# RWKV-7 chunk inverse in a trunk-step kernel: each level works on the 32 of 64 columns that it alters

## The chip, the cores and the metric

The kernel runs on one core of a Trainium2 chip. Five engines work side by side and meet only at semaphores: PE (TensorE, matrix products from SBUF into PSUM; its weight loads are listed as PEld), DVE (VectorE), ACT (ScalarE), POOL (GpSimd) and SP, which here only issues DMAs. The metric is the device time of one execution in microseconds; lower is better. The time before is the median of three runs.

## The reference, cut to what matters

The reference is one inference step of a two-layer hybrid trunk. Layer 1 mixes tokens with a bidirectional RWKV-7 scan and a Mamba-2 scan. The part that matters is the RWKV scan:

```python
def wkv_scan(r, w, kk, a, k, v, S0, reverse):
    ...
    def step(S, inp):
        r_t, w_t, a_t, b_t, k_t, v_t = inp
        sa = jnp.einsum('bhvk,bhk->bhv', S, a_t)
        S = S * w_t[:, :, None, :] + sa[..., None] * b_t[:, :, None, :] + v_t[..., None] * k_t[:, :, None, :]
        return S, jnp.einsum('bhvk,bhk->bhv', S, r_t)
    S, ys = lax.scan(step, S0.astype(f32), xs, reverse=reverse)
```

There are 8 heads of 64 channels, 640 tokens and two directions. All data is float32.

## The kernel before, in words

The token loop is not run token by token. The 640 tokens are cut into NC = 10 chunks of 64. Inside a chunk the effect of the tokens on one another is a 64x64 triangular matrix (a "gram", masked), and the chunk is solved by the inverse of identity minus that matrix. A job is one direction (d = n % 2) of one pair of heads (j = n // 2): 8 jobs, each with 10 chunks and 2 heads (e). The head decides which half of the partitions holds a matrix (ROWS), so the arrays that matter, X_ (the inverse), XT_ (its transpose) and V_ (a product), are 128 partitions x 10 chunks x 64 columns. The chunks are worked on in two groups g of 5, 320 columns each.

The inverse is built by doubling. Level 0 is read straight from the masked gram. Levels lev = 1 to 5 join neighbouring blocks of width w = 2 ** lev. One level of one group is four steps:

- piece "v" on PE (line 2413): V = gram x X, ten products of 64x64 by 64x64, into PSUM bank VT(g); then on DVE (line 2684) the result times the 0/1 mask wlev(d, lev), which keeps the blocks that this level fills in, into V_.
- piece "xt" on PE: for levels under 5 ten products XT x V that are accumulated onto XB(g) in PSUM (line 2422), and ten products V x XT into VT(g) (line 2426); then on ACT (line 2580) the whole of XB(g) is copied to X_, and on DVE (line 2689) VT(g) is added to XT_.

Every product helper call has the line of `mm`, L226, in the profile, so only the accumulated product has a line of its own (L2422). A float32 product shows as two pairs of a weight load and a matmul. The mask keeps in each level only columns whose place in a block of 2w is in one half: half of the 64 columns of V and X change, and the other half of the columns of XT.

The order of the work is written out by hand. `wkv_order` (line 2239) yields the pieces for all engines alike; each engine goes through the same list and does its share, so every engine's queue follows that order. Each job has 20 slots, v and xt of two groups for 5 levels. After each slot the table BESIDE adds pieces of the next job (`to` = 1: lora, scan, prod, vt, gram, atok, bktok, lkv, x0, which prepare it) and of the job before (`to` = -1: uw, phi, z, chain, yi, ye, which use its inverse). Line 2671 evicts and masks the gram on DVE, lines 2643 to 2662 are the prod pieces on DVE, lines 2786 and 2788 make level 0 of the next job on POOL, and line 2400 (x0) turns it into XB. L2722 is a step of the state chain on DVE. L2548, L2561, L2562 and L2568 are ACT's copies in the pieces prod, vt and atok. PE takes PSUM banks 4 to 6 in turn for the pieces beside the levels; `claim` waits until the bank has been read.

Constants come from one array in DRAM. `shape_constants` fills it on the host, `const_columns` gives its layout; SP loads four of them and the start state before the RWKV phase (lines 3087 and 3088), and DVE and POOL wait for 16 * 5 on wkv_loaded.

## Time and profile before

| | |
|---|---|
| median of 3 runs | 1996.38 us (1993.99 to 1997.78) |
| the profiled execution: span from first to last instruction | 2001.7 us; no other time is given for it |
| PE busy, share of the span | 1921.7 us, 96% |
| DVE busy | 1071.2 us, 54% |
| ACT busy | 717.5 us, 36% |
| POOL busy | 140.2 us, 7% |
| mean granted TensorE clock | 0.983 |

Busy time of an engine is time in which one of its instructions runs. Matmuls are pipelined, so busy PE time is not time at its peak rate. A group in a table is a line, an engine and an operation, with what it writes and reads and the shape as partitions x elements. The chain of waits is followed back from the last instruction, at each step to what released it.

### The profile page before, as it was taken

The numbers are of one execution on the slowest core, as the hardware profiler recorded it, in microseconds if no ns is written. First come the engines' busy times: TensorE is split into PE (matmuls) and PEld (weight loads), VectorE is DVE, ScalarE is ACT, GpSimd is POOL, SyncE is SP. The second block draws the span as 40 slices with busy tenths as digits, with TensorE's granted clock in tenths as the row PEclk, the third lists the DMA queues.
The fourth block names the chain that finished last, engine by engine and source line by source line (L and its number), as shares of the span: only waits on it lengthen the run. The fifth ranks groups of instructions, "written<-read, shape, count | busy, mean of one in ns | idle before, by whom it ended". The sixth has DMA issues, their size and how long they took to land.

```text
span 2001.7 us, 41374 instructions
## 1 busy us (share of the span) xinstructions
PE 1921.7 (96%) x18397; PEld 1700.8 (85%) x18397; DVE 1071.2 (54%) x1976; ACT 717.5 (36%) x1313; POOL 140.2 (7%) x138
## 2 busy tenths in 40 slices
PE   5998999999999999999999889999999999999997
PEld 2795444899999999999998678888659999999997
DVE  3226754475555563245475776766547555556223
ACT  2323554353333351133345744444214333334211
POOL 2000000000000000000001523322000000000000
PEclk7999999999999999999999999999899999999999
DMA  9123738312221223232221000000211222122322
GB/s 339 56 85 119 273 112 301 119 58 85 85 70 58 85 58 87 59 105 70 64 84 41 7 3 4 4 4 4 91 43 43 85 84 84 52 76 59 87 64 76
DMA packets 142065, 164.25 MB, mean 82 GB/s; under 512 B 2512, under 2 KB 107136, under 8 KB 141888
## 3 DMA queue, kind: packets, MB, share of 16 engines
q1 hardware_dynamic: 138736, 150.29, 23.3%
q0 software_dynamic: 3152, 11.32, 1.5%
q8 instruction: 145, 2.38, 0.5%
q14 instruction: 32, 0.26, 0.0%
HBM read 157.85 MB, written 3.75 MB: 81 GB/s over the span
## 4 chain that ended last, share of the span: by engine, by line
PE 87%; DVE 6%; DMA 2%; POOL 2%; ACT 1%; issue 1%; POOLq 0%; DVEq 0%; SPq 0%
PE ps L226 82%; DMA ring<-in_ada_w 2%; POOL work L2786 1%; PE ps L2422 1%; DVE ring L2671 1%; PE ps L1280 1%; DVE work L498 1%; POOL work L2788 1%; PE ps L347 1%; PE ps L2027 1%; DVE small L1415 0%; PE ps L2400 0%; PE ps L462 0%; DVE work L2689 0%; DVE work L2684 0%
## 5 line engine op out<-in xcount | busy, mean ns | idle before, releaser
L226 PE MATMUL ps<-x_hi_r,w_lo 128*128 128x320 f32 (+3 forms) x2240 | 519.7, 307 | 0.4 <-issue 0.4
L226 PE MATMUL ps<-x_hi_r,w_hi 128*128 128x320 f32 (+2 forms) x1792 | 428.9, 311 | 0.9 <-issue 0.9
L226 PE MATMUL ps<-x_lo_r,w_hi 128*128 128x320 f32 (+2 forms) x1792 | 424.9, 308 | 0.0
L226 PEld LDWEIGHTS ps<-x_hi_r,w_lo 128*128 128x128 f32 (+1 forms) x2240 | 372.4, 186 | 2.0 <-issue 0.5
L226 PEld LDWEIGHTS ps<-x_lo_r,w_hi 128*128 128x128 f32 x1792 | 305.6, 188 | 0.0
L226 PEld LDWEIGHTS ps<-x_hi_r,w_hi 128*128 128x128 f32 x1792 | 303.8, 188 | 1.4 <-issue 1.3
L226 PE MATMUL ps<-work 64*64 64x64 f32 (+9 forms) x3322 | 285.0, 281 | 17.0 <-ACT work L1344 6.7
L226 PEld LDWEIGHTS ps<-work 64*64 64x64 f32 (+5 forms) x3322 | 177.7, 152 | 97.6 <-issue 64.1
L678 DVE SCALAR_TENSOR_TENSOR work<-ps,par,work 128x511 f32<-128x511 f32 (+1 forms) x188 | 103.3, 550 | 254.5 <-ACT work L840 244.6
L840 ACT ACTIVATE work<-ps,par 128x640 f32<-128x640 f32 x88 | 78.0, 886 | 372.5 <-PE ps L226 372.5
L718 ACT ACTIVATE w_hi<-ring 128x1024 fp32r<-128x1024 f32 (+1 forms) x152 | 135.8, 938 | 206.9 <-DMA ring<-in_ffn_down 182.7
L729 DVE TENSOR_TENSOR w_lo<-ring,w_hi 128x1024 fp32r<-128x1024 f32 (+1 forms) x152 | 158.6, 1078 | 87.0 <-ACT w_hi L718 87.0
L226 PE MATMUL ps<-g_lo,w_hi 128*128 128x320 f32 (+2 forms) x704 | 174.6, 309 | 0.0
L226 PE MATMUL ps<-work,ring 64*64 64x64 f32 (+3 forms) x2368 | 122.0, 238 | 7.3 <-DVE work L2689 3.3
L226 PEld LDWEIGHTS ps<-g_lo,w_hi 128*128 128x128 f32 x704 | 121.4, 188 | 0.0
L226 PEld LDWEIGHTS ps<-work,ring 64*64 64x64 f32 (+2 forms) x2368 | 94.9, 142 | 30.8 <-issue 25.5
L448 DVE SCALAR_TENSOR_TENSOR h<-ps,mods,h 128x512 f32<-128x512 f32 (+2 forms) x76 | 34.9, 494 | 140.6 <-PE ps L226 140.5
L226 PE MATMUL ps<-x_lo_r,w_lo 128*128 128x320 f32 (+2 forms) x416 | 108.1, 310 | 0.0
L680 DVE SCALAR_TENSOR_TENSOR work<-ps,par,work 128x511 f32<-128x511 f32 (+1 forms) x188 | 103.4, 550 | 6.7
L226 PE MATMUL ps<-x_hi_r,w_in_hi 128*128 128x320 f32 (+1 forms) x384 | 88.4, 312 | 0.5 <-issue 0.4
L226 PE MATMUL ps<-x_lo_r,w_in_hi 128*128 128x320 f32 (+1 forms) x384 | 86.8, 307 | 0.0
L226 PE MATMUL ps<-ring,cond 128*32 128x512 f32 x384 | 56.0, 668 | 19.9 <-DMA ring<-in_ada_w 19.8
(383 smaller groups left out, 2534.1 us busy)
## 6 DMA issues: line engine op xcount, KB each, us to landing
ring<-in_ada_w SPq DMA_DIRECT2D x24, 2048.0 KB, 8.1
ring<-in_ffn_up SPq DMA_DIRECT2D x44, 1024.0 KB, 7.3
ring<-in_ffn_down SPq DMA_DIRECT2D x16, 1408.0 KB, 6.9
ring<-in_l_w_in SPq DMA_DIRECT2D x11, 1024.0 KB, 5.2
ring<-in_l_w_out SPq DMA_DIRECT2D x4, 2048.0 KB, 7.9
ring<-in_l_w_in SPq DMA_DIRECT2D x3, 2048.0 KB, 9.5
h<-in_xT POOLq DMA_DIRECT2D x1, 2560.0 KB, 14.7
out_yT<-work POOLq DMA_DIRECT2D x2, 768.0 KB, 4.0
```

The costliest lines, as they stand in the source:

```text
L226: return pe.matmul(out, lhsT, rhs, start=first, stop=last)
L347: ins = pe.matmul(ps_all[:, 1024 * pair + heads * c:1024 * pair + heads * c + heads], squares[:, P * c:P * c + P], col, start=first and c ...
L448: ins = dve.scalar_tensor_tensor(h(m, x, y), psum(u % 2, x, y), gate(m, c), h(m, x, y), ALU.mult, ALU.add)
L498: ins = dve.scalar_tensor_tensor(hn(t, x, y), h(t, x, y), gain(t, c), bank(6 + p)[:, x - a:y - a], ALU.mult, ALU.mult)
L678: ch(dve.scalar_tensor_tensor(acc(a + 1, b), psrc(a, b - 1), w0, acc(a + 1, b), ALU.mult, ALU.add))
L680: ins = dve.scalar_tensor_tensor(acc(a, b - 1), psrc(a + 1, b), w2, acc(a, b - 1), ALU.mult, ALU.add)
L718: act.activation(wh_b[:, SLOT * (f % 2) + w * part:SLOT * (f % 2) + w * part + w], ring[:, SLOT * (n % RING) + w * part:SLOT * (n % RING) ...
L729: dve.tensor_tensor(wl_b[:, at:at + w], ring[:, at:at + w], wh_b[:, SLOT * (f % 2) + w * part:SLOT * (f % 2) + w * part + w].bitcast(F32), ...
L840: act.activation(tile(cacc, 2 * (m % 2) + half), spair(n % 3, cut=up_cut(n)), ACT.Identity, bias=pc(f"ffn_b{l}", half * FT + m), scale=cw( ...
L1280: ins = pe.transpose(bank(4)[:, P * kt:P * kt + P] if kt < 4 else bank(5, P), pb[:, P * kt:P * kt + P], ident[:, :])
L2027: pe.matmul(out(hd), xtok[:, 512 * c + 64 * hd:512 * c + 64 * hd + 64], M_b[:, 1024 * x + P * hd:1024 * x + P * hd + P], start=hd % 4 < 2, ...
L2422: x = pe.matmul(XB(g)[p0:p1, c - 5 * g, :], XT_(n)[q0:q1, c, :], V_[q0:q1, c, :], start=False, stop=True, skip_group_check=True)
```

## The change

In each level the products, masks, additions and copies work on the half of the columns that the level alters, taken by a strided view: with w = 2 ** lev, 32 / w runs of w neighbouring columns, w apart. On V and X it is side d, on XT the other side. The other columns of V_ now keep old values. As the left operand of the products V is still loaded with all 64 columns, so rows of the V x XT product that belong to the other side hold values that must not be added; the addition therefore becomes one with a per-partition factor rsel(d, lev) of 0 or 1. V_ is set to zero once, before the first job. The constant rsel (10 columns) is new, with a DMA of its own, and the waits on wkv_loaded go to 16 * 6.

```diff
--- before.py
+++ after.py
@@ -65,7 +65,7 @@
     at, n = {}, 0
     for name, w in (("ident", P), ("blk", P), ("rotA", P), ("rotB", P), ("cosA", NL), ("sinA", NL),
                     ("cosB", NL), ("sinB", NL), ("gmask", 2 * P), ("wmask", 2 * P), ("wlev", 12 * 64),
-                    ("id64", 64), ("reset65", 650), ("reset", NT), ("sel6", 6 * P), ("rmask", 8)):
+                    ("id64", 64), ("rsel", 10), ("reset65", 650), ("reset", NT), ("sel6", 6 * P), ("rmask", 8)):
         at[name] = (n, w)
         n += w
     return at, n
@@ -2167,7 +2167,7 @@
         assert 2688 + 3 * NT + 4 * NT + 512 >= W0 + 4 * NT
         c_reset2, c_wmask, c_wlev, c_id64 = tk(650), tk(2 * P), tk(12 * 64), tk(64)
         assert 2688 + 3 * NT + 4 * NT + 512 + 650 + 2 * P + 13 * 64 <= W0 + 8 * NT
-        pv_b, _ = tk(36), tk(24)
+        pv_b, c_rsel, _ = tk(36), tk(10), tk(14)
         RH_b, X_b, XT_b = tk(4 * NT), tk(2 * NT), tk(2 * NT)
         cum_b, swx_b = tk(650), tk(650)
         V_b, W_b, RP_b, PH_b, ZP_b = tk(NT), tk(NT), tk(NT), tk(NT), tk(NT)
@@ -2189,6 +2189,14 @@
         V_, W_, RP_, PH_, ZP_ = c10(V_b), c10(W_b), c10(RP_b), c10(PH_b), c10(ZP_b)
         en65, ep65, sw65 = c10(en_b), c10(cum_b), c10(swx_b)
         wlev = lambda d, lev: c_wlev[:, 384 * d + 64 * lev:384 * d + 64 * lev + 64]
+        rsel = lambda d, lev: c_rsel[:, 5 * d + lev - 1:5 * d + lev]
+
+        def half_columns(ap, lev, side):
+
+            w = 1 << lev
+            if len(ap.shape) == 2:
+                return ap.rearrange("p (b h w) -> p b h w", h=2, w=w)[:, :, side, :]
+            return ap.rearrange("p c (b h w) -> p c b h w", h=2, w=w)[:, :, :, side, :]
         HALF5, THIRD = ((0, 5), (5, 10)), ((0, 4), (4, 8), (8, 10))
         ROWS = ((0, 64), (64, P))
         pv = lambda n, c, w=1: pv_b[:, 12 * (n % 3) + c:12 * (n % 3) + c + w]
@@ -2410,7 +2418,8 @@
                     for c in range(5 * g, 5 * g + 5):
                         for e in range(2):
                             (p0, p1), (q0, q1) = ROWS[e], ROWS[1 - e]
-                            ins = mm(pe, VT(g)[q0:q1, c - 5 * g, :], G_(n)[p0:p1, c, e, 0:64], X_(n)[p0:p1, c, :])
+                            ins = mm(pe, half_columns(VT(g)[q0:q1, c - 5 * g, :], lev, d), G_(n)[p0:p1, c, e, 0:64],
+                                     half_columns(X_(n)[p0:p1, c, :], lev, d))
                     ins.then_inc(sg("wkv_v"), 1)
                 elif kind == "xt":
                     lev, g = i
@@ -2419,11 +2428,13 @@
                         if lev < 5:
                             for e in range(2):
                                 (p0, p1), (q0, q1) = ROWS[e], ROWS[1 - e]
-                                x = pe.matmul(XB(g)[p0:p1, c - 5 * g, :], XT_(n)[q0:q1, c, :], V_[q0:q1, c, :],
+                                x = pe.matmul(half_columns(XB(g)[p0:p1, c - 5 * g, :], lev, d), XT_(n)[q0:q1, c, :],
+                                              half_columns(V_[q0:q1, c, :], lev, d),
                                               start=False, stop=True, skip_group_check=True)
                         for e in range(2):
                             q0, q1 = ROWS[1 - e]
-                            ins = mm(pe, VT(g)[q0:q1, c - 5 * g, :], V_[q0:q1, c, :], XT_(n)[q0:q1, c, :])
+                            ins = mm(pe, half_columns(VT(g)[q0:q1, c - 5 * g, :], lev, 1 - d), V_[q0:q1, c, :],
+                                     half_columns(XT_(n)[q0:q1, c, :], lev, 1 - d))
                     if lev < 5:
                         x.then_inc(sg("wkv_x"), 1)
                     ins.then_inc(sg("wkv_t"), 1)
@@ -2577,7 +2588,8 @@
                 elif kind == "xt" and i[0] < 5:
                     lev, g = i
                     act.wait_ge(sg("wkv_x"), 8 * n + 2 * (lev - 1) + g + 1)
-                    act.activation(X_(n)[:, 5 * g:5 * g + 5, :], XB(g), ACT.Copy).then_inc(sg("wkv_xu"), 1)
+                    act.activation(half_columns(X_(n)[:, 5 * g:5 * g + 5, :], lev, d), half_columns(XB(g), lev, d), ACT.Copy)\
+                        .then_inc(sg("wkv_xu"), 1)
                 elif kind == "uw":
                     act.wait_ge(sg("wkv_uw"), 3 * n + i + 1)
                     c0, c1 = THIRD[i]
@@ -2592,7 +2604,7 @@
                     act.activation(gates_b[i // 2][:, :], spair(i // 2 % 2), ACT.Copy).then_inc(sg("gate_read"), 1)
 
         def wkv_dve(dve, ch, scan_end):
-            dve.wait_ge(sg("wkv_loaded"), 16 * 5)
+            dve.wait_ge(sg("wkv_loaded"), 16 * 6)
             many = lambda ap, k: ap.unsqueeze(1).to_broadcast([P, k, ap.shape[1]])
             links = 0
             for kind, n, i in wkv_order():
@@ -2626,6 +2638,7 @@
                     dve.scalar_tensor_tensor(part, part, pc("gnorm", t), factor_b[:, a:a + 320], ALU.mult, ALU.mult)
                 elif kind == "x0" and n == 0 and i == 1:
                     ch(dve.memset(pv_b[:, 12:36], 1.0))
+                    ch(dve.memset(V_b, 0.0))
                 elif kind == "scan":
                     dve.wait_ge(sg("wkv_sw"), 2 * n + 2)
                     dve.tensor_tensor_scan(cum_b[:, :], c_reset2[:, :], swx_b[:, :], 0.0, ALU.mult, ALU.add)\
@@ -2681,12 +2694,16 @@
                 elif kind == "v":
                     lev, g = i
                     dve.wait_ge(sg("wkv_v"), 10 * n + 2 * (lev - 1) + g + 1)
-                    dve.tensor_tensor(V_[:, 5 * g:5 * g + 5, :], VT(g), many(wlev(d, lev), 5), ALU.mult).then_inc(sg("wkv_vm"), 1)
+                    mask = half_columns(wlev(d, lev), lev, d)
+                    dve.tensor_tensor(half_columns(V_[:, 5 * g:5 * g + 5, :], lev, d), half_columns(VT(g), lev, d),
+                                      mask.unsqueeze(1).to_broadcast([P, 5, mask.shape[1], mask.shape[2]]), ALU.mult)\
+                        .then_inc(sg("wkv_vm"), 1)
                 elif kind == "xt":
                     lev, g = i
                     dve.wait_ge(sg("wkv_t"), 10 * n + 2 * (lev - 1) + g + 1)
-                    x = XT_(n)[:, 5 * g:5 * g + 5, :]
-                    dve.tensor_tensor(x, x, VT(g), ALU.add).then_inc(sg("wkv_tu"), 1)
+                    x = half_columns(XT_(n)[:, 5 * g:5 * g + 5, :], lev, 1 - d)
+                    dve.scalar_tensor_tensor(x, half_columns(VT(g), lev, 1 - d), rsel(d, lev), x, ALU.mult, ALU.add)\
+                        .then_inc(sg("wkv_tu"), 1)
                 elif kind == "phi":
                     dve.wait_ge(sg("wkv_phi"), 3 * n + i + 1)
                     c0, c1 = THIRD[i]
@@ -2741,7 +2758,7 @@
         def wkv_pool(pool, store_scan):
             pl = Chain(pool, "pool_chain")
             pl.n = 1
-            pool.wait_ge(sg("wkv_loaded"), 16 * 5)
+            pool.wait_ge(sg("wkv_loaded"), 16 * 6)
             for kind, n, i in wkv_order():
                 j, d = n // 2, n % 2
                 if kind == "lora":
@@ -3083,7 +3100,7 @@
                     sp.dma_start(c_reset1, part_of_const("reset65")).then_inc(sg("reset_loaded"), 16)
                     sp.wait_ge(sg("ssd_tok"), 5)
                     sp.wait_ge(sg("ssd_skip"), 4)
-                    for name, to in (("reset65", c_reset2), ("wmask", c_wmask), ("wlev", c_wlev), ("id64", c_id64)):
+                    for name, to in (("reset65", c_reset2), ("wmask", c_wmask), ("wlev", c_wlev), ("id64", c_id64), ("rsel", c_rsel)):
                         sp.dma_start(to, part_of_const(name)).then_inc(sg("wkv_loaded"), 16)
                     sp.dma_start(s0_b, t_in["wkv0"]).then_inc(sg("wkv_loaded"), 16)
                     sp.wait_ge(sg("wkv_yi"), 2 * JOBS)
@@ -3146,6 +3163,7 @@
             lev.append(lower if (d == 0) != (b == 0) else upper)
     put("wlev", np.concatenate(lev, 1))
     put("id64", s == t)
+    put("rsel", np.concatenate([(s % (2 << b) >= (1 << b)) == (d == 1) for d in range(2) for b in range(1, 6)], 1))
     put("reset65", np.tile((np.arange(650) % 65 != 0)[None], (P, 1)))
     put("reset", np.tile((np.arange(NT) % P != 0)[None], (P, 1)))
     sel6, rmask = np.zeros((P, 6, P)), np.zeros((P, 8))
```

## Rows read from the trace of the kernel before

**Rows 1.** The page: busy time of PE, and the granted clock in 40 slices.

```profile
PE 1921.7 (96%) x18397; PEld 1700.8 (85%) x18397; DVE 1071.2 (54%) x1976; ACT 717.5 (36%) x1313; POOL 140.2 (7%) x138
...
PEclk7999999999999999999999999999899999999999
```

**Rows 2.** Busy time in stretches; after POOL: granted clock, DMA share, GB/s.

```profile
1261.00:1295.40 34.40, 32.50 (x983) 28.50 (x983) 23.88 (x58) 16.89 (x42) 9.92 (x7) 1.00 0.02 4
...
1231.90:1235.30 3.40, 3.40 (x62) 3.16 (x64) 1.39 (x4) 2.44 (x5) 0.00 (x0) 0.51 0.00 0
```

**Rows 3.** Chain of waits, 1261 to 1296 us: start us, us, what.

```profile
1262.92 0.40 DVE work L2689
...
1264.05 0.40 DVE work L2684
...
1267.57 0.32 ACT work L2580
...
1273.48 0.40 DVE work L2684
...
1274.07 0.39 DVE work L2689
...
1279.65 0.62 PE ps L2400 x14
```

**Rows 4.** Chain of waits, 1190 to 1400 us: L2647 in three jobs.

```profile
1226.98 0.74 DVE work L2647
...
1261.69 0.73 DVE work L2647
...
1295.79 0.73 DVE work L2647
```

**Rows 5.** Groups by line: duration ns min/median/max, starts; the second by form.

```profile
L2684 DVE TENSOR_TENSOR work<-ps,work x80: 460/491/494, 1146.7 to 1415.1; 128x320 f32<-128x320 f32 x80
...
L448 DVE SCALAR_TENSOR_TENSOR h<-ps,mods,h 128x128 f32<-128x128 f32 x44 | 14.1, 344 | 7.5 <-PE ps L226 7.4
...
L2580 ACT ACTIVATE work<-ps x64: 417/439/443, 1150.2 to 1413.6; 128x320 f32<-128x320 f32 x64
...
L2585 ACT ACTIVATE work<-ps x24: 278/385/387, 1181.3 to 1420.7; 128x256 f32<-128x256 f32 x16, 128x128 f32<-128x128 f32 x8
```

**Rows 6.** DVE in order of time: start us, us, line, operation.

```profile
1258.49 0.28 DVE L2694 TENSOR_TENSOR work<-ps,work 128x128 f32<-128x128 f32 x1
1258.69 0.28 DVE L2695 TENSOR_TENSOR work<-ps,work 128x128 f32<-128x128 f32 x1
```

**Rows 7.** PE and weight loads in order of time: start us, us, line, operation.

```profile
1218.15 0.14 PEld L2422 LDWEIGHTS ps<-work 64*64 64x64 f32 x2
...
1218.21 0.14 PEld L2422 LDWEIGHTS ps<-work 64*64 64x64 f32 x2
...
1439.12 1.20 PEld L347 LDWEIGHTS ps<-blk,sqb 128*128 128x128 f32 x10
...
1213.34 0.63 PE L226 MATMUL ps<-work,ring 64*64 64x64 f32 x15
1213.90 0.81 PE L226 MATMUL ps<-work 64*128 64x320 f32 x4
...
1202.26 1.16 PE L226 MATMUL ps<-work 64*128 64x128 f32 x16
1203.35 0.62 PE L226 MATMUL ps<-work,ring 64*64 64x64 f32 x14
```

**Rows 8.** SP's issues, one landing, and DVE at the phase's start, in order of time.

```profile
1092.34 2.02 SPq L3087 DMA_DIRECT2D work<-in_const  x4
...
work<-in_const SPq DMA_DIRECT2D x1, 32.0 KB, 3.9
...
1130.62 1.01 DVE L2618 SCALAR_TENSOR_TENSOR merged<-work,par,ps 128x384 f32<-128x384 f32 x2 [1.50 <-PE ps L2032]
...
1146.70 0.49 DVE L2684 TENSOR_TENSOR work<-ps,work 128x320 f32<-128x320 f32 x1 [2.66 <-PE ps L226]
```

## The prediction

> **What bounds the kernel now.** I read the page first, then the stretches of single jobs, then the chain of waits through one job, then single groups. The page says that PE is busy nearly all the time at nearly full clock [rows 1]. The reader should not stop there. The change touches only the level loop of the RWKV inverse, whose masks run from 1146.7 to 1415.1 us [rows 5], some 275 us or 14% of the span, for eight jobs. One job's stretch of 34.4 us has PE busy for 32.5 us and DVE for 23.9 us [rows 2], which still looks like a PE bound. The chain of waits through the same stretch says otherwise [rows 3]. From 1262.92 to 1279.65 us it runs over DVE (the prod pieces, with one L2689 and one L2684 queued among them), ACT (with one L2580), the gram products on PE, DVE again (L2684 and L2689 between two gram evictions) and POOL. Only from 1279.65 us on, where PE takes up x0 (L2400), is it PE alone, until the next prod stretch begins a little before the L2647 at 1295.79 us [rows 4], some 14 us. So a job is some 20 us of a mixed chain and 14 us of PE, and the change has to be priced in both. The start of one prod piece in successive jobs gives the pitch of a job: 34.71 and 34.10 us [rows 4].
>
> **Weights, masks and vector work, part by part.** Per job there are 5 levels and 2 groups: 10 masks (L2684), 10 additions (L2689), 8 copies (L2580), and 20 blocks of products.
>
> *Mask.* L2684 on 320 columns takes 491 ns [rows 5]. In the chain it advances the queue by 0.40 us [rows 3]. The same kind of operation on 128 columns takes 0.28 us and the next one starts 0.20 us later [rows 6]. From 128 to 320 columns the step grows by 0.20 us in 192 columns, 1.04 ns a column. 160 columns: 0.20 + 32 x 1.04 ns = 0.23 us of queue, 0.31 us long. Each mask gives 0.17 us.
>
> *Addition.* It becomes an operation with a per-partition factor. L448 is such an operation: 128 columns take 344 ns [rows 5] against 280 ns without the factor [rows 6], so the factor costs 64 ns. 160 columns: 0.29 us of queue. Each addition gives 0.11 us, not 0.17.
>
> *Copy.* L2580 takes 439 ns; another PSUM copy on ACT takes 278 ns at 128 and 385 ns at 256 columns [rows 5], 0.84 ns a column. 160 columns: 0.305 us. Each gives 0.13 us.
>
> All three now read and write runs of 2, 4, 8, 16 or 32 numbers. No row at hundreds of columns has runs so short. Bounds: at best nothing on top; at worst the halving is given back in full, for which the nearest rows are the 320-column ones. I take nothing on top: the 128-column rows read PSUM in runs of 64 out of 128 (lines 2694 and 2695) and still cost less per column than the contiguous 320 ones, so a gap between runs by itself is free. The Trainium skill (Vector Engine (DVE) Microarchitecture Reference, 5.2 Measured stream behaviour on trn2) has full rate for runs of at least two adjacent words that start on 8 bytes, and 1.3 to 2.5 ns a column otherwise. By it all runs here are free, level 1 included; no row here shows it.
>
> *Products.* Half the columns stream, but each product still loads 64 weight columns. Weight loads of a level block follow each other at 0.06 us (1218.15, 1218.21), and ten loads of 128 weight columns whose products have 2 columns take 1.20 us, 0.112 us each [rows 7]. So a load sets a pitch of its own of about 0.112 / 2 = 0.056 us for 64 weight columns even when almost nothing streams. The pitch inside a block should stay: zero for all 1600 passes (8 jobs x 5 levels x 2 groups x 5 chunks x 2 passes, for v and for xt). What does shrink is the end of a block before work of another tile shape. After 64-column products the next block starts 0.15 us after the last product's start (1213.34 + 0.63 - 0.22 = 13.75, then 13.90). After 128-column ones it is 0.20 us (1202.26 + 1.16 - 0.27 = 3.15, then 3.35) [rows 7]. That is 0.86 ns a column, so 27 ns less at 32 columns. By the order table about 9 of the 20 blocks stand before a piece of another shape (lora, atok, bktok, gram, a turned vt), about 3 of them in the stretch where PE alone is the chain: 0.08 us a job. Bounds: 0 and 9 x 27 = 0.24 us.
>
> *What is added.* A load of ten columns in SP's queue beside the four constant loads at 1092 us [rows 8]; DVE's first operation of this phase starts at 1130.62 us, so some 30 us cover it. If that cover were gone it would cost one landing, 3.9 us, once. The clearing of V stands in DVE's queue before the first mask, where DVE idles 2.66 us [rows 8]; it needs at most the 0.73 us of a 640-column operation such as L2647 [rows 4], and without that cover it costs just this. The queue waits for one semaphore more of the same DMA group; nobody else is behind it.
>
> **The sum.** On the chain of one job lie the addition just before the prod stretch and one inside it (2 x 0.11), one mask (0.17), one copy (0.13, in the three jobs of even number after job 0, whose chain it is; I did not find it on that of the odd ones), and one mask and one addition ahead of the last gram eviction (0.28, of which I take 0.20, because the eviction then waits for its product). With the PE term that is 0.22 + 0.17 + 0.20 + 0.08 = 0.67 us, and 0.80 us with the copy. Seven such stretches (three with the copy): 7 x 0.67 + 3 x 0.13 = 5.1 us. Job 0's first levels and the last job's tail, where levels follow one another with little beside them: 0.4 us. Total 5.5 us.
>
> Against it stands the clock. The chip granted 0.51 of full speed, the lower of its levels (1.2 of 2.4 GHz), for 3.4 us at 1231.9 us, just after a stretch in which PE had mostly waited for DVE [rows 2]. The job with that stretch is 34.71 us and the next one, without, is 34.10 us [rows 4]: some 0.6 us each time (the two jobs differ in direction, so this is rough). Halved streams leave PE less to do around these waits. I charge one more such stretch: 0.7 us. Net 4.8 us.
>
> The profiled execution's span is 2001.7 us; no other time of it is given. It lies 5.3 us above the median of 1996.4 us, so the sum reads 2001.7 - 4.8 = 1996.9 for it, and 1996.4 - 4.8 = 1991.6 us for the median. About 0.2% (4 us) is what a measurement of this kernel can tell from no change, and my sum lies just beyond that.
>
> **Rivals.**
>
> *Absorbed (chance 0.27).* The chain moves to what is late next: ACT's queue before the gram products, POOL's three long operations, the gram products themselves. None of these shrinks. For it: the piece before each saved one often waited for PE. Against it: the saved pieces stand on the chain itself [rows 3]. Only the additions and masks of the prod stretch would count, about 0.3 us in 7 jobs: 2 us, so 1994.4 us.
>
> *The clock takes it back (0.10).* If nearly every job gets two stretches of 3.4 us at the lower level, some 9 more than now, 9 x 0.6 = 5.4 us cancel the gain; twice that price gives 5 us too many: 1996 to 2001 us. For it: the kernel already falls there in some jobs. Against: before 1279.65 us PE is not the chain, so a slow clock costs little.
>
> *Strided products are slow (0.08, the slower side).* Place: the reads of the moving operand and the writes to PSUM in the 1600 passes. A pass has 0.059 us, and 32 columns at 0.86 ns need 0.028 us. So streaming at half rate would be hidden completely under the weight load. It decides from 0.059 + 5.5 / 1600 = 0.0624 us a pass, 1.95 ns a column, 2.3 times today's price. At four times (0.11 us a pass) it costs 1600 x 0.051 = 82 us: 2073 us. If only the runs of two (level 1, 320 passes) suffer, 16 - 4.8: 2008 us. No row shows a product on short runs. The PSUM page of the Trainium skill (PSUM — Partial Sum Buffer, Specifications (TRN2)) says that any non-contiguous access pattern slows matmuls significantly, with 8-byte lines. By its word this rival would be the forecast; by its 8-byte line a run of two is whole, and nothing is lost. No run yet shows which.
>
> *Products do halve (0.05).* That would be the full meaning of "32 of 64 columns": the weight load is not the limit, and a pass falls from 0.059 to about 0.04 us. In the 14 us of PE chain lie 9 blocks, 90 passes a job: 90 x 0.019 x 8 = 14 us more, 1978 us. Against it: the 2-column products at 0.112 us [rows 7].
>
> **How the numbers follow.** Forecast as summed: 0.50. Its own spread is 1988 to 1995 us (PE ends from 0 to 0.24 us a job, low-clock stretches from 0 to 4, short runs from free to half given back). About two thirds of it lie beyond 4 us. Faster: two thirds of 0.50, all of 0.05, and a third of the absorbed case, about 0.45. Slower: 0.08, a third of the clock case and a little for unknown costs, 0.13. The rest, 0.42, is within 0.2%. The range 1986.5 to 1998.5 takes in the forecast, the absorbed case and most of the clock case and leaves out the two extremes.
>
> **What the next profile would show.** Mask about 0.31 us, addition about 0.38 us, copy about 0.305 us, at every level alike; if level 1 is longer, short runs cost something. Weight loads inside level blocks still at 0.059 us; a larger pitch is the strided rival, a smaller one the last. Block ends at 0.12 instead of 0.15 us. Pitch of a job about 0.7 us shorter, the chain still over the prod pieces, gram and POOL. More stretches at half clock in the level loop speak for the clock rival. I am wrong if the three vector times are as said and the jobs are not shorter, or if the weight-load pitch moves at all.

## The result, and the profile after

The changed kernel takes 2012.2 us (median of 6, 2004.4 to 2028.7) against 1997.5 us for the kernel before (median of 6): a ratio of 1.0075, 95% interval 1.0047 to 1.0103. It is some 15 us slower, where 1991.6 us and a range up to 1998.5 us were forecast. The profiled execution took 2008.95 us, with a span of 2007.1 us.

The page of the kernel after, busy time and granted clock in 40 slices, beside [rows 1]:

```profile
PE 1932.5 (96%) x18397; PEld 1713.9 (85%) x18397; DVE 1053.3 (52%) x1977; ACT 709.1 (35%) x1313; POOL 140.0 (7%) x138
...
PEclk8999999999999999999999988988899999999999
```

DVE and ACT do less, as they should. PE, whose products shrank, is busy for 10.8 us more, and there are slices with an 8 in the clock in the level loop. The busy time of PE grew where the same instructions ran at a lower clock; in the jobs at full clock, below, it shrank a little (31.8 us against 32.2 in the second).

The changed groups by line of the kernel after, duration in ns min/median/max, beside [rows 5]:

```profile
L2698 DVE TENSOR_TENSOR work<-ps,work x80: 294/324/330, 1144.4 to 1420.7; 128x160 f32<-128x160 f32 x80
...
L2705 DVE SCALAR_TENSOR_TENSOR work<-ps,work x80: 369/384/387, 1148.0 to 1422.2; 128x160 f32<-128x160 f32 x80
...
L2591 ACT ACTIVATE work<-ps x64: 286/314/332, 1148.1 to 1419.1; 128x160 f32<-128x160 f32 x64
```

Mask, addition and copy have nearly the durations forecast (0.31, 0.38, 0.305 us), and the levels hardly differ: their means lie at 313 to 325, 379 to 384 and 302 to 321 ns, with 325, 384 and 320 ns at level 1, where the runs have 2 numbers. So short runs cost next to nothing. The vector side of the change did what it promises.

Now the loop by jobs, each window from the first mask of a job to the first of the next. First the kernel after, all eight jobs; after the length come the busy times of PE, PEld, DVE, ACT and POOL, then the granted clock, third from the end:

```profile
1144.40:1178.20 33.80, 29.21 (x792) 25.80 (x794) 19.24 (x42) 14.04 (x36) 12.36 (x13) 0.85 0.03 11
1178.20:1211.70 33.50, 31.78 (x969) 28.20 (x971) 21.93 (x58) 15.87 (x42) 9.88 (x7) 1.00 0.02 4
1211.70:1247.70 36.00, 33.51 (x958) 30.34 (x958) 22.01 (x59) 14.04 (x36) 11.79 (x9) 0.86 0.01 4
1247.70:1280.90 33.20, 31.60 (x969) 28.11 (x969) 21.06 (x57) 15.88 (x42) 9.88 (x7) 1.00 0.02 4
1280.90:1320.20 39.30, 37.60 (x958) 34.12 (x958) 22.06 (x58) 14.19 (x36) 11.79 (x9) 0.74 0.01 3
1320.20:1353.80 33.60, 31.76 (x969) 28.17 (x969) 21.09 (x57) 15.89 (x42) 9.89 (x7) 1.00 0.02 4
1353.80:1392.70 38.90, 36.74 (x962) 33.34 (x962) 22.14 (x58) 14.19 (x36) 11.79 (x9) 0.78 0.01 4
1392.70:1422.60 29.90, 25.77 (x768) 24.36 (x764) 13.59 (x42) 10.13 (x25) 4.61 (x3) 0.83 0.02 4
```

The same windows of the kernel before, the second to the sixth:

```profile
1179.50:1214.00 34.50, 32.20 (x969) 28.16 (x969) 24.34 (x57) 16.87 (x42) 9.92 (x7) 1.00 0.02 4
1214.00:1248.70 34.70, 31.87 (x958) 28.33 (x958) 24.13 (x58) 15.05 (x36) 11.82 (x9) 0.95 0.02 4
1248.70:1282.70 34.00, 32.10 (x969) 28.16 (x969) 23.54 (x56) 16.88 (x42) 9.92 (x7) 1.00 0.02 4
1282.70:1318.20 35.50, 33.05 (x958) 29.51 (x958) 24.11 (x58) 15.05 (x36) 11.84 (x9) 0.90 0.02 4
1318.20:1352.60 34.40, 32.23 (x969) 28.19 (x969) 23.69 (x57) 16.87 (x42) 9.91 (x7) 1.00 0.02 4
```

The pattern is plain once the clock column is read. Where the clock is 1.00 the jobs are shorter after: 33.5, 33.2 and 33.6 us against 34.5, 34.0 and 34.4. Where it isn't, they are longer: 36.0 against 34.7 and 39.3 against 35.5. Here is the lower clock by itself in the kernel after, with the stretch just before one fall:

```profile
1224.70:1228.10 3.40, 2.14 (x88) 1.84 (x82) 3.40 (x7) 0.32 (x1) 1.91 (x2) 1.00 0.00 0
1228.10:1238.30 10.20, 9.06 (x166) 8.36 (x166) 5.62 (x17) 2.22 (x5) 0.00 (x0) 0.50 0.01 3
1296.30:1316.80 20.50, 19.70 (x384) 18.04 (x384) 9.41 (x27) 5.39 (x14) 4.63 (x4) 0.50 0.01 3
1371.40:1388.50 17.10, 17.10 (x324) 15.75 (x326) 6.80 (x19) 4.98 (x13) 4.18 (x3) 0.50 0.01 3
```

In the kernel before, the stretch ahead of the fall in [rows 2], and its three other low stretches:

```profile
1228.50:1231.90 3.40, 1.63 (x66) 1.39 (x66) 3.40 (x9) 0.04 (x1) 1.68 (x2) 1.00 0.02 5
...
1156.80:1160.20 3.40, 3.36 (x94) 3.06 (x96) 1.77 (x4) 0.98 (x3) 0.00 (x0) 0.51 0.02 5
...
1300.20:1307.00 6.80, 6.32 (x100) 5.74 (x102) 3.78 (x12) 2.48 (x5) 0.00 (x0) 0.50 0.01 2
1402.60:1412.80 10.20, 8.14 (x151) 7.71 (x155) 3.17 (x8) 2.25 (x6) 1.83 (x2) 0.50 0.01 2
```

Before, the loop has 23.9 us at the lower level, in four stretches of 3.4, 3.4, 6.8 and 10.2 us. After, it has 68.3 us, in five stretches of 10.2, 10.2, 20.5, 17.1 and 10.2 us. In the third and fifth job the clock falls in the same place as before, where PE waits for DVE's prod pieces, and in the seventh it now falls there too; once low, it stays low for longer. And it stays so with PE listed as busy for 17.10 of 17.10 us: busy time of PE doesn't tell what the clock will do. Outside the loop the two profiles differ the other way, 42.7 us at the lower level before and 24.7 after, so their spans lie only 5.4 us apart, and their loops 7.6 us.

What a slow PE does to the chain is the last thing to see. Shares of the chain of waits by line, first the low stretch of the kernel after (1296.3 to 1316.8 us), then the same part of the job in the kernel before (1298 to 1318 us):

```profile
by line: PE ps L226 66.3%; PE ps L2431 9.7%; PE ps L2377 7.4%; PE ps L2359 7.1%; DVE work L2666 5.0%; DVE work L2669 3.6%; DVE work L2698 1.1%; DVE work L2675 0.5%; DVE work L2673 0.4%; issue 0.2%
```

```profile
by line: PE ps L226 33.6%; POOL work L2786 13.3%; DVE ring L2671 9.8%; POOL work L2788 7.8%; PE ps L2400 5.8%; PE ps L2422 5.7%; DVE work L2651 5.3%; DVE work L2653 4.3%; DVE work L2684 4.0%; PE ps L2369 4.0%; DVE work L2656 3.7%; DVE work 
```

Before, PE carries about half of this chain and POOL and DVE the rest, although the clock is low for 6.8 us of it. After, it is over 90% PE: the mixed chain has become a chain of slow products.

### The profile page after: what moved, and what is told of

It is laid out like the page before. It is cut to its first block, busy times and chain, and to the rows that moved or that the text cites. A ratio compares the mean times of both kernels' runs of the same rounds, so it can differ in the third digit from the quotient of the medians.

```text
span 2007.1 us, 41376 instructions
## 1 busy us (share of the span) xinstructions
PE 1932.5 (96%) x18397; PEld 1713.9 (85%) x18397; DVE 1053.3 (52%) x1977; ACT 709.1 (35%) x1313; POOL 140.0 (7%) x138
## 4 chain that ended last, share of the span: by engine, by line
PE 89%; DVE 6%; ACT 2%; DMA 1%; issue 1%; POOL 1%; POOLq 0%; DVEq 0%; SPq 0%; ACTq 0%
PE ps L226 83%; PE ps L2431 1%; DMA ring<-in_ada_w 1%; PE ps L1280 1%; DVE small L1415 1%; DVE work L498 1%; POOL work L2803 1%; PE ps L347 1%; PE ps L2027 1%; ACT work L1344 0%; DVE ring L2684 0%; PE ps L462 0%; PE ps L2408 0%; DVE work L2664 0%; DVE work L2666 0%
## 5 line engine op out<-in xcount | busy, mean ns | idle before, releaser
L226 PE MATMUL ps<-work 64*64 64x32 f32 (+10 forms) x3322 | 292.8, 288 | 16.5 <-ACT work L1344 7.6
L226 PEld LDWEIGHTS ps<-work 64*64 64x64 f32 (+5 forms) x3322 | 186.6, 161 | 96.5 <-issue 63.6
L226 PE MATMUL ps<-work,ring 64*64 64x32 f32 (+4 forms) x2368 | 125.6, 245 | 6.1 <-ACT work L384 2.9
L226 PEld LDWEIGHTS ps<-work,ring 64*64 64x64 f32 (+2 forms) x2368 | 100.3, 151 | 29.9 <-issue 26.2
```

The lines of the kernel that those rows point to most:

```text
L226: return pe.matmul(out, lhsT, rhs, start=first, stop=last)
```

## The experiments

The theory: fewer streamed columns leave the granted clock to fall more often and stay low longer around the waits for DVE, and this costs more than the shorter vector work gives. The rivals: the new vector work or the order that it brings causes the loss (A); products with short runs are slow in themselves (B).

All results in one table. "Low" is the time at the lower clock within the loop, from the first mask to the last addition in the profiled run, and "loop" the time of that loop; both come from one profile. "Clock" is the mean granted clock of whole executions, averaged over all the runs in the row, so it also tells whether the profile is typical. Each ratio is to runs of the kernel before that were made beside those in the row.

| kernel | median us (runs) | against before, 95% | loop us | low us | clock |
|---|---|---|---|---|---|
| before | 1997.5 (6), 1999.8 to 2000.4 beside the others | | 270.6 | 23.9 | 0.986 to 0.987 |
| after | 2012.2 (6) | 1.0075 (1.0047 to 1.0103) | 278.2 | 68.3 | 0.972 |
| after, again | 2014.3 (6) | 1.0070 (1.0049 to 1.0090) | 281.9 | 81.9 | 0.972 |
| both products full | 1995.2 (12) | 0.9978 (0.9966 to 0.9990) | 262.5 | 13.7 | 0.986 |
| both products full, again | 1996.3 (12) | 0.9981 (0.9969 to 0.9993) | 265.4 | 27.6 | 0.986 |
| v full | 2002.0 (12) | 1.0020 (1.0005 to 1.0034) | 270.5 | 44.7 | 0.981 |
| V x XT full | 2000.2 (12) | 1.0004 (0.9992 to 1.0016) | 266.5 | 30.7 | 0.981 |
| products half, masks and copies full | 2019.5 (6) | 1.0123 (1.0080 to 1.0166) | 289.0 | 95.6 | 0.966 |
| additions half alone | 1996.7 (12) | 0.9982 (0.9972 to 0.9993) | 265.7 | 17.1 | 0.987 |
| after, contiguous halves | 2022.5 (4) | 1.0098 (1.0070 to 1.0127) | 278.3 | 64.9 | 0.968 |
| after, filled off the gap | 2019.4 (5) | 1.0091 (1.0076 to 1.0107) | 279.9 | 47.8 | 0.974 |
| full products, filled off the gap | 2001.3 (11) | 1.0001 (0.9992 to 1.0011) | 271.3 | 17.1 | 0.987 |
| after, filled in the gap | 2002.1 (12) | 1.0006 (0.9988 to 1.0024) | 277.0 | 54.7 | 0.983 |
| full products, filled in the gap | 1994.4 (10) | 0.9965 (0.9951 to 0.9979) | 260.4 | 3.4 | 0.989 |

**Both products full.** The masks, additions and copies stay at 32 columns, and so does the accumulated product, since the other columns of V_ are stale.

```diff
-ins = mm(pe, half_columns(VT(g)[q0:q1, c - 5 * g, :], lev, d), G_(n)[p0:p1, c, e, 0:64],
-         half_columns(X_(n)[p0:p1, c, :], lev, d))
+ins = mm(pe, VT(g)[q0:q1, c - 5 * g, :], G_(n)[p0:p1, c, e, 0:64], X_(n)[p0:p1, c, :])
...
-ins = mm(pe, half_columns(VT(g)[q0:q1, c - 5 * g, :], lev, 1 - d), V_[q0:q1, c, :],
-         half_columns(XT_(n)[q0:q1, c, :], lev, 1 - d))
+ins = mm(pe, VT(g)[q0:q1, c - 5 * g, :], V_[q0:q1, c, :], XT_(n)[q0:q1, c, :])
```

> The kernel after, but the v product and the product that makes the next X transposed stream all 64 columns again; masks, additions and copies stay on 32, and so does the product that accumulates onto X. Clock theory (halving the streamed columns lets the granted clock fall in the prod stretches of the odd jobs and stay low for 10 to 20 us, which costs more than the shorter vector work gives): low clock in the level loop back to about 24 us as before (after: about 68), a job at full clock still about 0.9 us shorter than before, so 1988 to 1993 us, faster than both kernels, and mask, addition and copy at 0.32, 0.38 and 0.31 us. Rival A (the shorter vector operations and the order they bring cause the loss): about as after, 2006 to 2014 us, with low stretches as long as after. Rival B (products with runs of 2 to 32 columns are slow in themselves): also 1988 to 1993 us, but then the pitch of weight loads within a block would differ from after's 58 ns, which it should not by the clock theory.

Giving PE more columns makes the kernel 17 us faster than after and faster than before as well. At 1995.2 us it lies above the 1988 to 1993 us that I expected, although it has less low clock in the profile (13.7 us) than the 24 us that I allowed for. The third, fifth and seventh jobs of this kernel:

```profile
1214.10:1248.20 34.10, 31.57 (x958) 28.20 (x959) 21.91 (x59) 13.91 (x36) 11.78 (x9) 0.95 0.02 4
...
1281.50:1315.70 34.20, 31.50 (x958) 28.17 (x959) 21.85 (x58) 13.92 (x36) 11.77 (x9) 0.95 0.02 4
...
1349.00:1382.10 33.10, 30.27 (x960) 27.10 (x962) 21.81 (x57) 13.94 (x36) 11.79 (x9) 1.00 0.02 4
```

DVE and ACT have the same work as after (22.0 and 14.0 us in the third job), PE is the one that differs. Rival A is out: the shorter vector work is all there, and the loss is gone.

**One product full.** The first edit alone, then the second alone.

> The kernel after, but the v product streams 64 columns; the other two stay at 32. Clock theory: between after and the kernel with both full, 30 to 60 us of low clock in the level loop, 1994 to 2006 us. Rival A: as after, 2006 to 2014 us. Rival B: between, with the pitch of v blocks different from that of the others.

> The kernel after, but the product that makes the next X transposed streams 64 columns; the v product and the accumulated one stay at 32. Clock theory: like the kernel with the v product full, 30 to 60 us of low clock, 1994 to 2006 us; the two together tell whether one product's columns are enough to keep the clock up. Rival A: as after, 2006 to 2014 us. Rival B: between, with the pitch of these blocks different from that of the v blocks.

Both lie between, as expected: 2002.0 and 2000.2 us with 44.7 and 30.7 us of low clock. More columns give less low clock and less time, and in the mean clock of all runs the steps are 0.972, 0.981 and 0.986; the accumulated product was on 32 columns in all of them.

**Half products alone.** Masks and copies as before; the addition on 160 columns without a factor.

```diff
-act.activation(half_columns(X_(n)[:, 5 * g:5 * g + 5, :], lev, d), half_columns(XB(g), lev, d), ACT.Copy)
+act.activation(X_(n)[:, 5 * g:5 * g + 5, :], XB(g), ACT.Copy)
...
-dve.scalar_tensor_tensor(x, half_columns(VT(g), lev, 1 - d), rsel(d, lev), x, ALU.mult, ALU.add)
+dve.tensor_tensor(x, half_columns(VT(g), lev, 1 - d), x, ALU.add)
```

(and the mask as at L2684 of the kernel before)

> Only the three products stream 32 columns. Masks and copies work on 320 columns as before; additions work on 160 without the factor. Masks at about 0.49 us and copies at 0.44 us again. Clock theory: as much low clock as after, 50 to 90 us in the level loop, and jobs at full clock as long as before (about 34.3 us), so slower than after by 2 to 5 us: 2012 to 2020 us. Rival A (vector work is the cause): about as before, 1994 to 2000 us, with about 24 us of low clock. Rival B (strided products are slow): slower than before by all of it, about 2020 us, with a pitch over 58 ns at full clock.

The slowest kernel by its ratio, at the upper end of what I expected, with more low clock (95.6 us) than I allowed for. So thin products lose the clock with long vector work as well. Its first three jobs:

```profile
1148.80:1189.00 40.20, 36.02 (x792) 32.23 (x794) 20.48 (x41) 15.17 (x36) 12.37 (x13) 0.66 0.03 9
1189.00:1229.20 40.20, 38.19 (x969) 34.26 (x971) 23.09 (x58) 16.98 (x42) 9.87 (x7) 0.79 0.01 3
1229.20:1267.80 38.60, 36.27 (x958) 32.94 (x958) 22.94 (x58) 15.12 (x36) 11.77 (x9) 0.78 0.01 3
```

Whether long vector work beside thin products is worse than short isn't shown: the intervals of this kernel (1.0080 to 1.0166) and of after (1.0047 to 1.0103) overlap. I had also said that its jobs at full clock would be as long as before; the only one is 33.3 us. One job is too little to lean on, and the additions were halved here too, so I tried these by themselves.

**Half additions alone**, in the kernel before.

```diff
-x = XT_(n)[:, 5 * g:5 * g + 5, :]
-dve.tensor_tensor(x, x, VT(g), ALU.add)
+half = lambda ap: ap.rearrange("p c (b h w) -> p c b h w", h=2, w=w)[:, :, :, 1 - d, :]
+x = half(XT_(n)[:, 5 * g:5 * g + 5, :])
+dve.tensor_tensor(x, x, half(VT(g)), ALU.add)
```

> The kernel before, in which only the additions work on 160 columns, without a factor: about 0.32 us instead of 0.49. Products, masks and copies on all columns. In the kernel with half products and half additions a job at full clock took 33.3 us, as in those with half masks and copies too, against 34.4 before. If the additions carry most of the vector gain: jobs at full clock about 33.4 us, low clock 10 to 30 us in the level loop, 1991 to 1995 us. If it is the sum of all three, as I added up (0.22 of 0.67 us for the additions): jobs at 34.1 us, 1995 to 1998 us.

This kernel has the vector work of the one with half products; its three level products stream 64 columns instead of 32. The times are 1996.7 and 2019.5 us, with 17.1 and 95.6 us of low clock: a second pair that differs in the products alone, but for the clearing and the small load. The time fits the sum of all three (the second reading): jobs at full clock take 34.0, 33.7 and 34.2 us, 0.3 us less than before (34.5, 34.0, 34.4), against 0.9 us with masks and copies too. By the medians the additions alone already bring most of the gain, 0.18% of the 0.19 to 0.22%; by the loops of the profiles, 265.7 us against 262.5 and 265.4, it is between half of it and nearly all. The intervals are wide against these differences, so the split stays rough. These additions have no factor: they take 322 ns, those of after 384 ns.

**Contiguous halves.** Same count and size of everything, no strides. At levels 1 to 4 these are not the columns that the level alters, so this kernel does not compute the inverse.

```diff
-            w = 1 << lev
+            w = 32
```

> The kernel after, but at every level the halves are 32 columns in one run instead of runs of 2, 4, 8 or 16, so it computes something else than the inverse from level 1 to 4. Same count, sizes and order of the work. Clock theory: as after, 50 to 90 us of low clock in the level loop, 2004 to 2020 us, pitch of weight loads in a block 58 ns, mask 0.32, addition 0.38 and copy 0.31 us. Rival B (short runs are slow): 1988 to 1994 us, with shorter masks or a smaller pitch.

As slow as after (1.0098 against 1.0075, intervals overlap; the median is a little above what I expected), with 64.9 us of low clock. So strides aren't the cause. The pitch of weight loads says the same. Weight loads of the kernel after within a level block, first at full clock, then at the lower; start us, us:

```profile
1222.22 0.14 PEld L2431 LDWEIGHTS ps<-work 64*64 64x64 f32 x2
...
1222.28 0.14 PEld L2431 LDWEIGHTS ps<-work 64*64 64x64 f32 x2
...
1230.35 0.23 PEld L2431 LDWEIGHTS ps<-work 64*64 64x64 f32 x2
...
1230.46 0.23 PEld L2431 LDWEIGHTS ps<-work 64*64 64x64 f32 x2
```

From one row to the next it is 0.06 us at full clock, as in [rows 7], and 0.11 us at the lower. Products in short runs are no slower here, and rival B is out. The Trainium skill (PSUM — Partial Sum Buffer, Specifications (TRN2)) says that any non-contiguous pattern slows matmuls significantly; in this case the runs don't agree with it for runs of 2 to 32 numbers, as far as they can tell: a product's stream has room under its weight load (by the prediction's estimate 0.028 us of 0.059), so a slowdown below about twofold would not show in the pitch.

**Filling the waits.** The direct test of the clock as cause is to add work to PE and see whether it gets faster. The first try added six products of the identity by itself to each job from job 1 on: four ahead of PE's wait in the piece turn, two ahead of the one in gram.

```diff
+            if i == 0 and n > 0:
+                for _ in range(4):
+                    pe.matmul(bank(to)[:, 0:P], ident[:, :], ident[:, :], start=True, stop=True, skip_group_check=True)
             pe.wait_ge(sg("wkv_spread"), n + 1)
```

> The kernel after with six products of the identity by itself added in each job from job 1 on, where PE waits for the vector engines: four before it waits for the spread of the next job (a gap of 1.36 us at 1229 us in the kernel after) and two before it waits for the first gram product's operand. They write a bank that the next instruction overwrites and nobody reads them. At full clock they take about 0.22 us each, 0.9 and 0.45 us, inside the waits. Clock theory, with low activity in these waits as what starts the fall: low clock in the level loop falls from about 68 us to 20 to 50 us, 1993 to 2006 us, faster than after by 5 us or more. Against: if the fall is due to the blocks before the waits alone, the low clock stays at 50 to 90 us and the time is that of after or up to 8 us above it, since the added work costs double at the low clock.

> The same six products added to the kernel with both products on 64 columns and masks, additions and copies on 32. Clock theory: low clock in the level loop from 14 us down to 0 to 10 us; against the kernel without them (1995.2 us) between 3 us less and 2 us more, 1992 to 1997 us. Against: where the waits are no longer empty because the vector work is shorter, the added work lies on the path, 8 x up to 1.3 us: up to 2005 us.

The first missed: 2019.4 us instead of 1993 to 2006, although the low clock of its profile, 47.8 us, lies in the 20 to 50 us that I expected. The second missed too, with 2001.3 us and 17.1 us of low clock instead of 1992 to 1997 and 0 to 10; only its reading "on the path, up to 2005 us" fits. I had put the gap of 1.36 us down to the wrong wait. It belongs to the turned a columns (L2377, piece atok), and the new products stood on the path: with both products full the jobs at full clock grew from 33.5, 33.3 and 33.3 us to 34.6, 34.1 and 33.9, some 0.8 us each, or 5.5 of the 6 us between 1995.2 and 2001.3 if all seven jobs grew alike, with hardly more low clock than without it (17.1 against 13.7 us). The whole loop of this profile is 8.8 us longer. A misplaced filling costs time, and with full products it gives no clock back. The second try fills the gap itself, and only for the jobs of odd n, which puts it into the first, third, fifth and seventh window:

```diff
+                    if i == 0 and d == 1:
+                        for _ in range(5):
+                            pe.matmul(bank(banks[0])[:, 0:P], ident[:, :], ident[:, :], start=True, stop=True, skip_group_check=True)
                     if i == 0:
                         pe.wait_ge(sg("wkv_prod"), n + 1)
```

(in the piece atok; the banks are claimed ahead of it)

> The kernel after with five products of the identity by itself in the odd jobs only, in the wait of PE ahead of the turned a columns (a gap of 1.36, 0.92 and 1.35 us in jobs 3, 5 and 7 of the kernel after, which is where the low clock begins). The earlier filling stood elsewhere and lay on the path; this one lies in the gap itself, 1.1 us at full clock. If the emptiness of this wait starts the fall: low clock in the level loop from 65 to 68 us down to 10 to 40 us, 1994 to 2006 us. If the thin blocks around it suffice for the fall: low clock 45 us or more, 2008 to 2020 us.

> The kernel after once more, on the chip of the filled one, so that the two are compared there. Clock theory: 2004 to 2025 us, 50 to 90 us of low clock in the level loop.

On the same chip 2014.3 us (2010.8 to 2020.1) became 2002.1 us (1992.1 to 2010.8): 20 products more, of which nobody reads the result, and 12 us less. The profiled run was the slowest of its twelve, so its 54.7 us of low clock are more than typical (its mean clock is 0.975; the median of the twelve is 0.9825, that of after again 0.973). Low time worked out from the mean clocks (twice the share that is missing from 1, times the execution) is some 68 us for the twelve runs and 114 us for after again. At the 0.30 us per us found below, 46 us less are worth 14 us, and 12 us were measured. Even in this profile some windows are shorter. The filling in the third job, and the windows of the third, fifth and seventh:

```profile
1232.97 2.29 PE L2372 MATMUL ps<-ident 128*128 128x128 f32 x9
```

```profile
1216.50:1250.40 33.90, 32.37 (x968) 29.23 (x969) 21.87 (x59) 13.92 (x36) 11.78 (x9) 0.95 0.02 4
...
1286.40:1320.10 33.70, 31.34 (x968) 28.24 (x968) 22.06 (x59) 13.92 (x36) 11.78 (x9) 1.00 0.02 4
...
1353.70:1394.10 40.40, 39.14 (x970) 35.67 (x972) 22.09 (x59) 14.19 (x36) 11.77 (x9) 0.75 0.01 3
```

36.0 and 39.3 us became 33.9 and 33.7. The seventh fell as before and the fourth fell anew (36.0 us long, with 6.8 us of low clock), and the second forecast of this run (45 us or more of low clock) holds for this one profile, though not its time. So the filled kernel has less low clock, and long low stretches still occur. How the filling does it isn't shown. In the first, third and seventh window the clock had already fallen, at 1161.1, 1232.7 and 1369.3 us, when the filling began, at 1165.4, 1233.0 and 1370.6 us. It then took 2.5 us instead of the 1.4 us at full clock in the fifth, and the low stretch ended 2.5, 3.1 and 19.2 us after the filling had begun. In this profile no fall can be said to have been prevented by the products in its own wait.

The same filling with both products full, and that kernel again without it:

> The same five products in the odd jobs, added to the kernel with both products on 64 columns (2 stretches of 3.4 us of low clock in the middle jobs). If the filling holds the clock: 7 us of low clock or less ahead of the last job, 1993 to 1996 us. If it doesn't: as without it or up to 3 us more, 1995 to 1999 us.

> The kernel with both products on 64 columns and the vector work on 32 once more, on the same chip: 1993 to 1997 us, 10 to 20 us of low clock in the level loop, faster than the kernel before by 0.1 to 0.35%.

1994.4 against 1996.3 us, and 0.35% faster than the kernel before: the lowest median of all, though its interval overlaps that without the filling. The repeat without it had 27.6 us of low clock, more than the 10 to 20 that I expected and twice that of the first profile (13.7). With the filling there were 3.4 us, none of them ahead of the last job. The windows of the filled kernel's third, fifth and seventh job show the clock whole:

```profile
1215.20:1248.10 32.90, 31.31 (x968) 28.03 (x968) 21.88 (x58) 13.94 (x36) 11.77 (x9) 1.00 0.01 4
...
1281.40:1314.80 33.40, 31.77 (x968) 28.32 (x966) 21.95 (x57) 13.93 (x36) 11.79 (x9) 1.00 0.02 4
...
1348.50:1381.40 32.90, 31.31 (x970) 28.10 (x972) 21.87 (x58) 13.91 (x36) 11.78 (x9) 1.00 0.02 4
```

## Why the prediction was wrong

**What the change gives at full clock: right.** Take the seven unfilled profiles with halved masks, additions and copies (after twice, both full twice, v full, V x XT full, contiguous). Their loop times lie on a line against their low-clock times: 257.6 us + 0.30 x low, the worst 1.1 us off. (The five without the two of after give 257.3 us + 0.31 x low, and for after's 68.3 and 81.9 us that makes 278.6 and 282.9 us, where 278.2 and 281.9 were measured. So what sets after apart from them is its low clock.) At the same slope the kernel before would take 270.6 - 0.30 x 23.9 = 263.4 us with no low clock. The halved work is therefore worth 5.8 us, give or take the 1 us by which single profiles leave the line; my sum said 5.5, of which some 0.6 us came from a term that failed (next paragraph). The additions by themselves, without the factor, give 263.4 - (265.7 - 0.30 x 17.1) = 2.9 us. By my 0.17 us for an addition without the factor, two a job over seven stretches make 2.4 us, so that term holds as far as this can tell. What additions with the factor give by themselves, 0.11 us each in my sum, no run shows.

**Products cost the same: right.** The pitch is unchanged, and the strided rival, the rival with halved passes and the page's rule (within the limit said above) all fall. Only the small term failed: I expected 27 ns less at the end of a block. Matmuls of the kernel after, the end of a block and the next of another shape:

```profile
1274.29 0.58 PE L226 MATMUL ps<-work,ring 64*64 64x32 f32 x14
1274.80 0.53 PE L2359 MATMUL ps<-ident,work 64*128 64x64 f32 x10
```

The last product starts at 1274.29 + 0.58 - 0.22 = 1274.65, the next shape at 1274.80: still 0.15 us. That was 0.08 us a job, some 0.6 us in all.

**Added load and clearing: nothing speaks against it.** They were forecast as hidden. In the twelve profiles that have them the first mask stands between 1143.2 and 1149.3 us, before at 1146.7 us [rows 5]; a cost below this scatter would not show.

**The clock: wrong, and it decides.** The step that failed is "I charge one more such stretch: 0.7 us". By the line the low clock cost 13 us in the profile of after and 17 us in the repeat. Three parts of it were wrong. The number: the loop has 44 us more at the lower level in the profile of after (68.3 - 23.9) and 58 us more in the repeat, 13 to 17 stretches of the length that I counted in, not one. Already before, two of the four stretches were longer than the 3.4 us of [rows 2]. The price: 0.30 us lost per us at the lower level, 1.0 us for 3.4 us instead of 0.6. The reason, which was the worst: "before 1279.65 us PE is not the chain, so a slow clock costs little." PE at half clock becomes the chain, as the shares by line show. Together: -5.8 + 0.30 x 44.4 = +7.5 us, and the two loops differ by 278.2 - 270.6 = 7.6 us (the line went through this point, so that is no test of it; the line without after's profiles, above, is). With the repeat's 58 us it is -5.8 + 17.4 = +11.6 us, and 281.9 - 270.6 = 11.3 us was measured. The medians are a little further apart still, 14 to 15 us. The profiled execution of after is the second fastest of its six, and the mean clock of the six goes from 0.980 in the fastest (2004.4 us) to 0.965 in the slowest (2028.7 us). Over whole executions, clocks of 0.972 and 0.987 stand for some 112 and 52 us at the lower level; 60 us more at 0.30 less the 5.8 us make +12 us, an estimate that takes the loop's price for the rest too.

The rival "The clock takes it back" had the mechanism, at a chance of 0.10. It allowed nine more stretches at 0.6 us each, 5.4 us, or twice that, and it counted stretches as if each ended by itself. The range ended at 1998.5 us because of it. In hindsight [rows 2] held the warning: the clock fell just after PE had waited, in a kernel where the change takes work from PE in these very blocks and leaves all waits where they are.

**What stays open.** Why the low clock lasts 3.4 us in one job and 20.5 us in another with the same instructions wasn't settled: the first job of after took 33.8 us with 10.2 us of it, and 39.8 us with 27.3 us in the repeat. The order and count of PE's work are the same in both. How far the full products alone could be pushed (the accumulated one on 64 columns needs a clean V_) wasn't tried, nor was the filling in the kernel before. Why products with fewer columns bring the low clock at all is told by no run; that they do is shown with short vector work (after against both full) and with longer (products half, masks and copies full, against additions half alone).

## What to carry to other kernels

Where weight loads set the pitch of small products, fewer moving columns save nothing on PE, and here they cost the clock: halve the vector work and leave the products full. Read the granted clock in every stretch with waits, and price a fall by the chain that would result with PE at half speed, not by today's chain. Work added in a wait of PE can pay: 20 products in the gap took 12 us off, while 42 products, six in each of seven jobs and off the gap, cost some 6 us in the kernel with full products.

## What was unexpected of the hardware

- Added products made a kernel 12 us faster (2014.3 to 2002.1 us). The Trainium skill (TensorE: Matmul & The Clock Gate, Part 1) tells of the lower clock as the state of an idle engine; here it held for 17.1 us with PE listed as busy for all of them.
- Each us at the lower level cost 0.30 us in the loop. The same page (Terms) puts the penalty of throttled time at half of it; by that, an estimate, the 44.4 us more would have cost 22 us instead of the 13 that the line gives. Part of the chain is not PE's and doesn't slow down with it: the masks of levels 4 and 5 take 320 and 325 ns at the lower level, 315 and 325 ns at full clock.
- A PSUM operation in runs of two numbers costs nearly what one in runs of 32 does: mask, addition and copy take 325, 384 and 320 ns on average at level 1, and in the kernel with contiguous halves 324, 384 and 305 ns (medians).
